# A second home for an expert's gate weights: expert 3's load ahead of expert 0's products

## What is computed

```python
def _grouped_moe(u, router_w, router_b, w_gate, w_up, w_down):
    ...
    expert_idx = g_sel[:, None] * EXPERTS_PER_GROUP + i_top      # 2 of 16 experts for each token
    ...
    h = jax.nn.silu(jnp.einsum('td,edf->tef', t, w_gate)) * jnp.einsum('td,edf->tef', t, w_up)
    h = h * combine[..., None].astype(h.dtype)
    out = jnp.einsum('tef,efd->td', h, w_down)
```

## Time and profile before

| | us |
|---|---|
| median of 3 runs | 749.99 (748.46 to 750.07) |
| the profiled execution's own time | 750.24 |
| its span, from the first instruction to the last | 748.4 |
| PE busy | 656.9 (88%) |
| DVE, ACT, POOL busy | 341.8, 230.8, 99.8 |
| experts, first gate product to last down product | 447.2 to 714.9 |

### The profile page before, as it was taken

How to read it: one execution, slowest core, us unless ns; L and a number is a source line. 1 busy time by engine, 2 the same in 40 slices (tenths; PEclk the granted TensorE clock), 3 DMA queues, 4 the chain that set the end, 5 groups by cost and what they waited for, 6 DMA issues and landing times.

```text
span 748.4 us, 15552 instructions
## 1 busy us (share of the span) xinstructions
PE 656.9 (88%) x6011; PEld 428.5 (57%) x6012; DVE 341.8 (46%) x660; ACT 230.8 (31%) x479; POOL 99.8 (13%) x185
## 2 busy tenths in 40 slices
PE   3698999997999799999999669799999979999910
PEld 0366665675777577777788455355555544555500
DVE  0445444266788776666756774211111111111117
ACT  0424433458654454545510401011111101111113
POOL 0220001020000000000000023122222211222241
PEclk9999999999999899999999959899999999999975
DMA  9999766294211222213697977999999999991147
GB/s 329 375 296 307 254 224 225 85 320 123 86 57 56 85 85 75 66 58 95 219 416 284 400 280 294 419 418 416 419 419 417 418 419 418 418 389 43 42 129 228
DMA packets 83882, 189.13 MB, mean 253 GB/s; under 512 B 7388, under 2 KB 60092, under 8 KB 68488
## 3 DMA queue, kind: packets, MB, share of 16 engines
q1 hardware_dynamic: 67664, 148.66, 52.7%
q0 software_dynamic: 7376, 32.26, 12.7%
q10 hardware_dynamic: 8808, 7.76, 3.1%
HBM read 174.58 MB, written 14.07 MB: 252 GB/s over the span
## 4 chain that ended last, share of the span: by engine, by line
PE 64%; DMA 14%; DVE 10%; ACT 5%; issue 3%; SPq 1%; POOL 1%; ACTq 0%; POOLq 0%; DVEq 0%
PE psum L1521 18%; PE psum L1532 9%; PE psum L1320 7%; PE psum L1321 7%; PE psum L1322 7%; DMA raw<-in_w_in_dram 4%; DMA wu<-in_moe_w_up_dram 4%; DMA x_sb<-in_x_dram 3%; PE psum L1504 2%; PE psum L1277 2%; PE psum L1511 2%; DMA x<-in_x_dram 2%; PE psum L1363 2%; PE psum L1391 1%; PE psum L1375 1%
## 5 line engine op out<-in xcount | busy, mean ns | idle before, releaser
L1521 PE MATMUL psum<-wg,xs 128*32 128x256 f32 x1280 | 152.6, 392 | 6.4 <-DMA wu<-in_moe_w_up_dram 5.6
L1521 PE MATMUL psum<-wu,xs 128*32 128x256 f32 x1280 | 152.6, 392 | 0.0
L1320 PE MATMUL psum<-uh,whi 128*128 128x512 f32 x336 | 138.7, 413 | 3.8 <-DVE wlo L893 3.8
L1321 PE MATMUL psum<-ul,whi 128*128 128x512 f32 x336 | 132.1, 393 | 0.0
L1322 PE MATMUL psum<-uh,wlo 128*128 128x512 f32 x336 | 131.8, 392 | 0.0
L1521 PEld LDWEIGHTS psum<-wg,xs 128*32 128x32 f32 x1280 | 73.1, 113 | 62.0 <-issue 6.8
L813 ACT ACTIVATE hsil<-psum 64x256 f32<-64x256 f32 x40 | 15.0, 375 | 231.7 <-PE psum L1521 231.7
L893 DVE TENSOR_TENSOR wlo<-raw,whi 128x1024 fp32r<-128x1024 f32 x42 | 51.4, 1224 | 72.5 <-ACT whi L638 72.1
L1200 DVE TENSOR_TENSOR h_sb<-psum,hsil 64x256 f32<-64x256 f32 x40 | 17.1, 428 | 136.7 <-ACT hsil L813 136.7
L1320 PEld LDWEIGHTS psum<-uh,whi 128*128 128x128 f32 x336 | 63.7, 190 | 25.6 <-issue 7.7
L1532 PE MATMUL psum<-wd,hT 128*32 128x256 f32 x1280 | 77.4, 382 | 0.7 <-DVE hT L1206 0.7
(11 more groups left out here) (251 smaller groups left out, 810.6 us busy)
## 6 DMA issues: line engine op xcount, KB each, us to landing
wg<-in_moe_w_gate_dram SPq DMA_DIRECT2D x32, 1024.0 KB
wu<-in_moe_w_up_dram SPq DMA_DIRECT2D x32, 1024.0 KB
wd<-in_moe_w_down_dram SPq DMA_DIRECT2D x32, 1024.0 KB
raw<-in_w_in_dram SPq DMA_DIRECT2D x42, 512.0 KB, 4.0
ada<-in_ada_w_dram POOLq DMA_DIRECT2D x16, 1024.0 KB, 5.9
ada<-in_ada_w_dram SPq DMA_DIRECT2D x8, 1024.0 KB, 14.7
y_d<-ysb ACTq DMA_DIRECT2D x160, 32.0 KB
y_d<-zrow POOLq DMA_DIRECT2D x8, 512.0 KB, 6.5
```

What stands on the lines that cost most here:

```text
L1320: mmul(bank[s % 2], h[:, k, :], uh[:, k, :], start=(k == 0), stop=False)
L1321: mmul(bank[s % 2], h[:, k, :], ul[:, k, :], start=False, stop=False)
L1521: ins = mmul(psum[32 * g:32 * g + 32, 0, 0:256], xs[:, k % 2, k // 2, :], wgu[slot][g // 2][:, k, (g % 2) * 256:(g % 2) * 256 + 256], star ...
```

## The change

One more 16 KB home is used: `R_A`, once the router's tables are dead. Expert 0's gate stays in `R_Q` (`wg_first`); the gates of experts 3, 6, 9, 12 and 15 go to `R_A`. Since experts 0 and 3 no longer share a gate home, expert 3's gate is issued when the router is done, ahead of expert 0's products. Later gates of slot 0 are issued as before when the expert three places earlier has used its own, but both gate halves now go ahead of both up halves. `idx` and `ctrl`, which are read through the whole expert part, move out of `R_A`. `g2r` and `be2r` move to `R_Q`, and their loads behind the last expert's. A new semaphore `route_done` says that DVE's last read of the router's tables is over.

```diff
-        idx = route("idx", [P, TCOL], U32)
-        ctrl = route("ctrl", [P, NUM + 1], I32)
...
+        wg_first = wgu[0][0]
+        wgu[0][0] = at(R_A, "wg0_later", [P, KT, FF])[0]
...
+        idx, o = at(o, "idx", [P, TCOL], U32)
+        o = (o + 31) // 32 * 32
+        ctrl, o = at(o, "ctrl", [P, NUM + 1], I32)
...
-        g2r, _ = at(R_A + 8 * KB, "g2r", [P, D])
-        be2r, _ = at(R_A + 12 * KB, "be2r", [P, D])
+        g2r, _ = at(R_Q, "g2r", [P, D])
+        be2r, _ = at(R_Q + 4 * KB, "be2r", [P, D])
...
             sp.wait_ge(S["ctrl_done"], 1)
             sp.wait_ge(S["wcol_ps"], 1)
+            sp.wait_ge(S["route_done"], 1)
+            for half in range(2):
+                piece(3, 0, 0, half)
...
+                sp.wait_ge(S["gu_ps"], last + 1)
+                for half in range(2):
+                    if slot > 0:
+                        piece(e, slot, 0, half)
+                    piece(e, slot, 1, half)
+                sp.wait_ge(S["d_ps"], last + 1)
+                load_down(sp, e, slot)
...
-            chain(V.tensor_copy(yrow[:, :, :], yrf[:, :, :]))
+            V.tensor_copy(yrow[:, :, :], yrf[:, :, :]).then_inc(S["route_done"], 1)
+            dve.wait_ge(S["route_done"], 1)
...
-            gate_up(0, 0, 32)
+            gate_up(0, 0, 32, first=True)
```

More of the change, by code:

```diff
@@ L324, in hybrid_layer @@
         b1r, o = at(o, "b1r", [P, D])
+        idx, o = at(o, "idx", [P, TCOL], U32)
+        o = (o + 31) // 32 * 32
+        ctrl, o = at(o, "ctrl", [P, NUM + 1], I32)
         assert o <= R_T + 38 * KB
-        g2r, _ = at(R_A + 8 * KB, "g2r", [P, D])
-        be2r, _ = at(R_A + 12 * KB, "be2r", [P, D])
+        g2r, _ = at(R_Q, "g2r", [P, D])
+        be2r, _ = at(R_Q + 4 * KB, "be2r", [P, D])
         fsum = small("fsum", [P, NT, 3])
-        fin = [[at(home + 4 * KB * i, f"fin{i}{j}", [P, D])[0] for j, home in enumerate((R_Q, R_U + 16 * KB, R_Y))]
+        fin = [[at(home + 4 * KB * i, f"fin{i}{j}", [P, D])[0] for j, home in enumerate((R_A, R_U + 16 * KB, R_Y))]
                for i in range(NT)]
@@ L370, in hybrid_layer @@
             fin_z fin_s fin_sqrt xT_m_ps xgs_rdy xs_rdy gu_ps silu_done h_done_m
-            hT_ps hT_sb d_ps y_ev fin_n fin_out v_ps v_sb idn_done pool_in t_done a2_done""".split()
+            hT_ps hT_sb d_ps y_ev fin_n fin_out v_ps v_sb idn_done pool_in t_done a2_done route_done""".split()
         S = {n: sem(n) for n in names}
@@ L465, in _ @@
             sp.wait_ge(S["y_lo"], KT)
-            load_gate_up(sp, 0, 0, 0)
-            load_gate_up(sp, 0, 0, 1)
+            for half in range(2):
+                ks = slice(4 * half, 4 * half + 4)
+                sp.dma_start(wg_first[:, ks, :], wg_v[0][:, ks, :]).then_inc(gu_in[0][half], 16)
+                sp.dma_start(wgu[0][1][:, ks, :], wu_v[0][:, ks, :]).then_inc(gu_in[0][half], 16)
             load_down(sp, 0, 0)
@@ L502, in _, with last_block @@
             sp.wait_ge(S["wcol_ps"], 1)
-            sp.dma_start(g2r[:, :], ln2_g[0].partition_broadcast(P)).then_inc(rows_in, 16)
-            sp.dma_start(be2r[:, :], ln2_b[0].partition_broadcast(P)).then_inc(rows_in, 16)
+            sp.wait_ge(S["route_done"], 1)
+            for half in range(2):
+                piece(3, 0, 0, half)
+            def last_block(i):
+                return sp.value_load(ctrl[0:1, i], min_val=0, max_val=NBLK - 1)
             def refill(e, slot, last):
                 sp.wait_ge(S["gu_ps"], last + 1)
-                load_gate_up(sp, e, slot, 0)
-                load_gate_up(sp, e, slot, 1)
+                for half in range(2):
+                    if slot > 0:
+                        piece(e, slot, 0, half)
+                    piece(e, slot, 1, half)
                 sp.wait_ge(S["d_ps"], last + 1)
@@ L515, in _ @@
                 for slot in range(NSLOTS):
[L516 to L519, removed]
+                    refill(3 * trip + slot, slot, last_block(bass.ds(3 * trip + (LAST + slot - 3), 1)))
+                last = last_block(bass.ds(3 * trip + LAST, 1))
+                sp.wait_ge(S["gu_ps"], last + 1)
+                for half in range(2):
+                    piece(3 * trip + 3, 0, 0, half)
+            refill(15, 0, last_block(slice(LAST + 12, LAST + 13)))
+            sp.dma_start(g2r[:, :], ln2_g[0].partition_broadcast(P)).then_inc(rows_in, 16)
+            sp.dma_start(be2r[:, :], ln2_b[0].partition_broadcast(P)).then_inc(rows_in, 16)
             for t in range(NT):
@@ L1513, in h_transpose, with gate_up @@
                 ins.then_inc(S["hT_ps"], 1)
-            def gate_up(b, slot, landed=None):
+            def gate_up(b, slot, landed=None, first=False):
+                gate = wg_first if first else wgu[slot][0]
                 pe.wait_ge(S["xs_rdy"], b + 1)
@@ L1521, in gate_up @@
                         ins = mmul(psum[32 * g:32 * g + 32, 0, 0:256], xs[:, k % 2, k // 2, :],
-                                   wgu[slot][g // 2][:, k, (g % 2) * 256:(g % 2) * 256 + 256],
+                                   (gate, wgu[slot][1])[g // 2][:, k, (g % 2) * 256:(g % 2) * 256 + 256],
                                    start=(k == 0), stop=(k == KT - 1))
@@ L1534, in down, with more_blocks @@
                 ins.then_inc(S["d_ps"], 1)
-            def more_blocks(first, more, slot, landed):
+            def more_blocks(first, more, slot, landed, of_first=False):
                 with pe.If(more > 0):
@@ L1540, in more_blocks @@
                         h_transpose(b - 1)
-                        gate_up(b, slot)
+                        gate_up(b, slot, first=of_first)
                         x_transpose(b + 1)
@@ L1549, in _ @@
             more = pe.value_load(ctrl[0:1, MORE:MORE + 1], min_val=0, max_val=NOVER)
-            more_blocks(0, more, 0, 32)
+            more_blocks(0, more, 0, 32, of_first=True)
             with pe.Fori(0, 5) as trip:
```

## The result

| | before | after |
|---|---|---|
| median of 9 runs each, us | 749.11 (745.72 to 750.07) | 743.27 (740.81 to 747.68) |
| ratio | | 0.9939, 95% interval 0.9911 to 0.9966 |
| profiled execution, us | 750.24 | 744.63 |
| its span | 748.4 | 742.8 |

The change made the kernel faster by about 0.6%, and the forecast of 745.1 us lies 1.8 us above the median of the changed kernel and 0.5 above its profiled execution. Two more sets of runs gave 0.9932 (0.9912 to 0.9953) and 0.9956 (0.9931 to 0.9981). The kernel before itself had medians from 746.75 to 749.11 in the four sets.

A forecast was written before the change was run, and what follows sets the result against it. The prediction took the full DMA queue to bound the expert part up to expert 12's half 1, then PE. Queue 3.5 plus clock 1.26 + 0.32 gave 5.1 us off 750.24, so 745.1 us, range 743.0 to 747.8.

The forecast's parts named there:

- The bound: Expert part: full DMA queue sets the pace until expert 12's half 1 lands at 619.17, then PE's own work.
- The queue's gain: DMA queue ahead of expert 12's half 1: two early gate transfers, 5.6 us, less the hole; taken as 3.5 us.
- the hole: DMA queue after expert 3's two up pieces, before its down ramps up: lost queue time, 2.1 us.
- no hole: Rival at expert 3's down: queue still warm, gains the full 5.6 us, time 743.0; chance 0.12.
- a longer lag: Low end at expert 3's down: start lag half as long again, queue gains only 1.7 us.
- Half 0 later by a piece: Experts 6, 9, 12, 15: half 0 complete after three pieces instead of two, 2.80 us later; half 1 unchanged in order.
- The clock stays up: Block 25: PE waits 1.5 us, then 0.9, too short to lower its clock; silu at 617.7.
- the code gap at expert 3: PE's unexplained 4.29 us gap before 477.96, first skipping expert 2's further-blocks loop, with no wait for data.
- its vanishing: Rival: without the 4.29 us gap PE waits longer, clock falls, gain only 2.8 to 3.7; 746.0 to 747.8 has 0.24.
- The clock term: Blocks 25 and 26: PE's clock no longer falls, saving 1.26 + 0.32 us.
- The things at nothing: `route_done`, SP's extra register load, the later `g2r` and `be2r` loads and moved tiles cost nothing.
- The slower rival: PE's first skip, just after 453.4: early gate still moving, PE could lose 5.9 us, time 752.6; chance 0.07.

The follow-up runs named there:

- late_gate: Changed kernel, but expert 3's gate is issued behind expert 0's products as before the change; ratio to the kernel before 0.9993.
- quiet_skip: Changed kernel with one more wait on SP, holding expert 4's transfers back until PE is past the skip to expert 3; ratio to the kernel before 1.0063.
- fill_hole: Changed kernel with PE's first expert-loop trip written out and a second home for slot 0's down, so expert 3's down follows its up; ratio to the kernel before 0.9954.
- half_early: Changed kernel with only gate half 0 of expert 3 issued early, half 1 behind expert 0's products; ratio to the kernel before 0.9976.
- pairs: Changed kernel with gate and up of experts 6, 9, 12, 15 again issued in turn, expert 3's gate early; ratio to the kernel before 0.9963.
- rows_last: Kernel before with only the loads of `g2r` and `be2r` moved behind the last expert's; ratio to the kernel before 1.0014.
- fill_hole_looped: Changed kernel with fill_hole's second home for down, PE's expert loop whole again and a branch for the down product; ratio to the kernel before 0.9979.

## Why the prediction was right, point by point

**The bound.** Right: the queue, not the homes, up to expert 12's half 1, and PE after it. late_gate and quiet_skip show it from both sides, and fill_hole shows the other regime: without the waits, PE's pace sets the end, and the homes are freed late.

**The queue's gain.** Right in kind, off in size: 4.28 us (165.52 - 161.24) where the sum had 3.5. The term that was mis-sized is the hole, 2.1 in the sum and 5.59 - 4.28 = 1.31 net. Down was issued 7.50 us after up's first piece, not 7.85 as before, since PE's small gap in block 1 (0.33) did not appear; and counted back from 613.42 over 54 pieces, down started effectively at 462.4, 2.7 us after its issue instead of 3.35. The down transfers came into a queue that had moved data until a moment before, and the lag was shorter. Between the two ends I gave, no hole (5.6) and a longer lag (1.7), 4.28 lies well inside. The prediction's figure from the Trainium skill (DMA: Bandwidth & Descriptors, Anatomy of one DMA) stands there for transfers issued by POOL, so for these, which SP issues, it was only an estimate. The sum rightly went by the trace's 2.80 us (16.78 us for six).

**Half 0 later by a piece.** Right: the distance between expert 12's halves was 5.43 us before and is 3.02 now, 2.4 less where the count said 2.8.

**The clock stays up.** This step failed. I had PE wait 1.5 us ahead of block 25, and it waited 2.95. It came 2.6 us earlier than I had put: block 24's silu is 152.87 us after block 0's, and I had 157.08 - 1.66 = 155.4. The reason is the code gap at expert 3, 2.63 instead of 4.29 us, with the half clock behind it: block 4 took 10.32 us instead of 12.92. I had called this gap unexplained and made its vanishing a rival that costs 1.6 us. It shrank by 1.66 us, and the clock did fall, but at the head of the block, where most of the cost lies in front of the landing anyway. The windows of the two halves in the changed kernel:

```profile
610.40:613.42 3.02, 3.02 (x32) 1.29 (x32) 0.00 (x0) 0.00 (x0) 0.00 (x0) 0.60 1.02 413
613.42:615.91 2.49, 2.49 (x37) 1.22 (x34) 0.00 (x0) 0.00 (x0) 0.00 (x0) 0.79 1.02 424
```

In half_early and pairs, where the code gap stayed above 4 us, block 24's silu came 154.90 and 155.36 us after block 0's, near my 155.4; the clock stayed at 1.00 through block 25's second half, and the silu came 2.0 us after the landing. So the step fails with the size of the code gap, which the prediction had no way to tell. In the changed kernel the silu came 2.49 us after the landing; I had 2.00, and before it was 3.26. The clock term is 0.77 + 0.32 = 1.09 us where the sum had 1.58. What is left of it is owed to where PE stands and not, as I had it, to short waits: late_gate has 0.87 + 0.33 us of it at the old landing. Together 4.28 + 1.09 = 5.37 us against 5.1. The two errors, +0.78 and -0.49, pulled in opposite directions: it is in part luck that the sum came out this close.

**The things at nothing.** Right. `route_done` cost nothing (SP issued 0.04 us before DVE's copy behind the old wait began, at 444.47), rows_last and late_gate show the rest, and the row loads had landed by 671 to 675 (DMA share 0.04).

**The slower rival.** It did not come. The early gate was through by 452.5 (0 GB/s from there to 453.0) and PE passed the first skip as before:

```profile
453.02 0.42 PE L1527 MATMUL psum<-cst,h_sb 64*128 64x64 f32 x2 [0.69 <-DVE h_sb L1216]
```

That such a gap depends on the DMA engines is real, as quiet_skip shows. That a later or larger early gate would have opened one at this skip is likely, and no run had it.

## What to carry to other kernels

When a DMA queue is full up to the last wait that matters, count the queue back from that wait in pieces: what is taken out of it ahead of the wait comes off the end, less the hole that its absence opens (here 2.60 of 2.80 us for the first piece, 1.68 for the second). Look for room before the stretch begins, and for a home that is free there. Before filling the last hole, ask what stands next: here it was PE's own pace with its code gaps, within a microsecond or two.

## What the hardware showed that was not expected

- PE's gap at its first skip to expert 3 depends on how busy the DMA engines are: 0.23 us with the queue standing, 2.5 to 4.5 us with it full at 418 GB/s and PE's original loop, and 1.15 us there and 5.62 at expert 4 with the code of fill_hole_looped. The Trainium skill (Runtime: NRT & Kernel Launch, Instruction fetch mechanics) says that a taken branch to a page that is not held forces a DMA fetch before PE can go on. The traces agree: an instruction transfer of 16 KB stands at this place in all twelve, and PE goes on 2.2 to 2.4 us after its end. That queue q8 is PE's is inferred from this fit. Why the fetch starts earlier or later among kernels with the same PE code (gaps of 2.53 to 4.54) stays open.
- Code that PE has run once stays at hand: neither the kernel before nor the changed one has a transfer on q8 between 489 and 709 us, where PE goes through the same loop body again and again, and PE has no such gap there.
- Where PE stands matters more than how long. At the same landing (165.5 us) the silu came 3.26 us after it with a wait of 3.5 us in the middle of the block (kernel before), and 2.39 us after it with one of 3.0 us ahead of the block (late_gate); with the clock up it is 2.00. PE ran at 1.2 GHz behind both waits, but in the second case most of the slow stretch lay ahead of the landing.
